# Key and input units of the near half as two spans of 264 columns

## What is computed

```python
h_res = jnp.concatenate([meta_b, x], axis=1)              # 16 + 1024 rows
h = rms_norm(h_res, pre_mix_g)
proj = jnp.einsum('bld,dc->blc', h, w_in)
q1, q2, k1, k2, v, u = jnp.split(proj, ...)
q1, q2, k1, k2 = partial_rope(...)                        # rotary positions
o = diff_attention(q1, q2, k1, k2, v, lam)                # causal, 4 heads
y = s5_ssm(u, ...)                                        # state space model over all 1040 rows
```

## Time and profile before

| | |
|---|---|
| median of 3 runs | 3443.7 us (3434.99 to 3446.54) |
| profiled execution, first to last instruction | 3446.0 us; of the three run times none is marked as its own, the slowest is 3446.54 |
| PE busy | 3106.2 us, 90% of the span |
| POOL, DVE, ACT busy | 1991.6, 1673.5, 854.1 us |
| near projection of `qk` units | about 77 to 182 us from the span's start |
| heads stage | about 182 to 510 us |

### The profile page before, as it was taken

How to read it: one execution, slowest core, us unless ns; L and a number is a source line. 1 busy time by engine, 2 the same in 40 slices (tenths; PEclk the granted TensorE clock), 3 DMA queues, 4 the chain that set the end, 5 groups by cost and what they waited for, 6 DMA issues and landing times.

```text
span 3446.0 us, 47777 instructions
## 1 busy us (share of the span) xinstructions
PE 3106.2 (90%) x19536; PEld 2393.9 (69%) x19536; DVE 1673.5 (49%) x2264; ACT 854.1 (25%) x1591; POOL 1991.6 (58%) x1076
## 2 busy tenths in 40 slices
PE   6987878799998879989999989998999988999997
PEld 4765646577776657767777767776777766788875
DVE  5844543444442551666656553646565564222333
ACT  3111123322221341123332223122323332100012
POOL 5820322554654656746665747755666765677872
PEclk9888889899999989999999999998999999999998
DMA  4343323222222434322221244332222222332231
GB/s 154 114 130 97 102 71 110 89 68 80 74 68 80 141 133 151 104 74 74 84 81 59 84 153 140 118 95 74 84 71 85 79 71 68 128 98 92 92 104 55
DMA packets 158027, 329.99 MB, mean 96 GB/s; under 512 B 34960, under 2 KB 74064, under 8 KB 157808
## 3 DMA queue, kind: packets, MB, share of 16 engines
q1 hardware_dynamic: 58752, 213.94, 19.2%
q10 hardware_dynamic: 99056, 112.99, 10.2%
HBM read 281.89 MB, written 44.97 MB: 95 GB/s over the span
## 4 chain that ended last, share of the span: by engine, by line
PE 76%; DVE 15%; ACT 3%; ACTq 2%; issue 2%; DMA 1%; POOL 0%; DVEq 0%
PE ps L1814 31%; PE ps L1855 12%; PE ps L1843 12%; PE ps L1665 2%; DVE acc_dense L2250 2%; PE ps L1576 2%; PE ps L1546 1%; DVE act_lo L2250 1%; DVE xn_dense L2257 1%; DVE ffh_lo L2930 1%; PE ps L2049 1%; DVE added L2250 1%; ACTq L965 1%; PE ps L1586 1%; PE ps L1693 1%
## 5 line engine op out<-in xcount | busy, mean ns | idle before, releaser
L559 POOL TENSOR_TENSOR w_hi<-w_raw,ones 128x1024 fp32r<-128x1024 f32 x408 | 805.6, 1975 | 1175.9 <-DMA w_raw<-weights 1172.7
L561 POOL TENSOR_TENSOR w_lo<-w_raw,w_hi 128x1024 fp32r<-128x1024 f32 x408 | 1019.3, 2498 | 32.0
L1814 PE MATMUL ps<-act_hi,w_hi 128*128 128x512 f32 x1696 | 703.9, 415 | 13.6 <-ACT qk_raw L674 8.1
L1814 PE MATMUL ps<-act_lo,w_hi 128*128 128x512 f32 x1696 | 678.4, 400 | 0.0
L1814 PE MATMUL ps<-act_hi,w_lo 128*128 128x512 f32 x1696 | 674.5, 398 | 0.0
L1814 PEld LDWEIGHTS ps<-act_hi,w_hi 128*128 128x128 f32 x1696 | 324.1, 191 | 108.5 <-issue 16.6
L1814 PEld LDWEIGHTS ps<-act_hi,w_lo 128*128 128x128 f32 x1696 | 323.7, 191 | 75.0
L1814 PEld LDWEIGHTS ps<-act_lo,w_hi 128*128 128x128 f32 x1696 | 324.1, 191 | 67.0 <-issue 1.7
L2250 DVE TENSOR_TENSOR acc_dense<-acc_dense,ps 128x512 f32<-128x512 f32 x352 | 242.0, 688 | 227.9 <-PE ps L1843 179.0
L1843 PE MATMUL ps<-w_hi,ffh_hi 128*128 128x512 f32 x704 | 296.1, 421 | 55.9 <-DVE acc_dense L2250 54.4
L1843 PE MATMUL ps<-w_hi,ffh_lo 128*128 128x512 f32 x704 | 282.4, 401 | 0.0
(11 more groups left out here) (371 smaller groups left out, 4389.1 us busy)
## 6 DMA issues: line engine op xcount, KB each, us to landing
w_raw<-weights SPq DMA_DIRECT2D x408, 512.0 KB, 3.5
rw<-rw_t ACTq DMA_DIRECT2D x24, 256.0 KB, 2.4
rw<-lora_t ACTq DMA_DIRECT2D x24, 256.0 KB, 2.0
row<-x ACTq DMA_DIRECT2D x8, 512.0 KB, 3.9
row_dense<-x ACTq DMA_DIRECT2D x8, 512.0 KB, 5.5
row_mix<-res ACTq DMA_DIRECT2D x8, 512.0 KB, 7.5
res<-row_mix ACTq DMA_DIRECT2D x8, 512.0 KB, 5.0
acc_dense<-res ACTq DMA_DIRECT2D x8, 512.0 KB, 5.6
```

What stands on the lines that cost most here:

```text
L559: pool.tensor_tensor(w_hi[:, s], raw, ones[:, 0:1].to_broadcast([P, 1024]), MUL).then_inc(w_hi_made, 1)
L561: pool.tensor_tensor(w_lo[:, s], raw, w_hi[:, s].bitcast(F32), SUB).then_inc(w_ready, 1)
L1814: mm = pe.matmul(out, ws[w][:, s, P * k:P * k + P], acts[a][:, k, x], start=(k, w, a) == (0, 0, 0), stop=(k, w, a) == (KT - 1, 1, 0))
```

## The change

`SPANS` has four entries: near 512, far 512 and two new ones of 264 columns, (0, 264) and (264, 528), that together are meta and near. Keys and inputs use spans 2 and 3 in place of 0 and 2. `rotate` and `rope_span` follow with the same spans; the count of items and steps doesn't change. In the heads stage each of the new products is two pieces of 12 matmuls, so a `u` unit's near part has 4 pieces in place of 5, and the stage has 81 pieces in place of 85.

```diff
-    SPANS = ((META, META + BANK), (META + BANK, L), (0, META))
-    spans_of = lambda m: (0, 2) if m >= 4 else (0,)
+    CUT = NEAR // 2
+    SPANS = ((META, NEAR), (NEAR, L), (0, CUT), (CUT, NEAR))
+    spans_of = lambda m: (2, 3) if m >= 4 else (0,)
+
+    def turned_beside(m, s):
+        before = spans_of(m - 1) if m else ()
+        if len(before) == 1:
+            return before if s == spans_of(m)[0] else ()
+        return tuple(b for b in before if b == s)
...
-    FAR = [("u", m, s) for m in range(4) for s in (0, 2)] + ...
-    FAR_PIECES = sum(1 if s == 2 else 4 for _, _, s in FAR) + 1
+    FAR = [("u", m, s) for m in range(4) for s in (2, 3)] + ...
+    far_pieces = lambda s: 2 if s >= 2 else 4
+    FAR_PIECES = sum(far_pieces(s) for _, _, s in FAR) + 1
...
-                if kind == "qk" and m and s in spans_of(m - 1):
-                    rotate(m - 1, s)
+                if kind == "qk":
+                    for before in turned_beside(m, s):
+                        rotate(m - 1, before)
...
-            for k in range(KT) if s == 2 else range(2 * part, 2 * part + 2):
+            each = KT // far_pieces(s)
+            for k in range(each * part, each * part + each):
```

More of the change, by code:

```diff
@@ L157, in build @@
     ROPES = len(PROJ) - QK_STEP
-    FAR = [("u", m, s) for m in range(4) for s in (0, 2)] + [("u", m, 1) for m in range(4)] + [("v", i, 1) for i in range(HALF, NT)] + [("qk", m, 1) for m in range(8)]
+    FAR = [("u", m, s) for m in range(4) for s in (2, 3)] + [("u", m, 1) for m in range(4)] + [("v", i, 1) for i in range(HALF, NT)] + [("qk", m, 1) for m in range(8)]
     FAR_U = 12
-    FAR_PIECES = sum(1 if s == 2 else 4 for _, _, s in FAR) + 1
+    far_pieces = lambda s: 2 if s >= 2 else 4
+    FAR_PIECES = sum(far_pieces(s) for _, _, s in FAR) + 1
     def ends_unit(kind, m, s):
@@ L184, in rope_index @@
     def rope_index(m, s):
-        return m + max(0, m - 4) + s // 2
+        return m + max(0, m - 4) + (s == 3)
     TB, TG, TQ = 8, 4, 2
@@ L749, in project @@
                 else:
-                    if m >= 2 and s == 0:
+                    if m >= 2 and s == spans_of(m)[0]:
                         store_turned(m - 2)
@@ L772, in project_far @@
                     store_far(m - 2)
-                if s != 2:
-                    for part in range(3):
-                        yield
+                for part in range(far_pieces(s) - 1):
+                    yield
                 if kind == "u":
@@ L778, in project_far @@
                         load_inputs(m - 1)
-                    if s != 2:
+                    if s != 3:
                         spills_landed(m % 2)
@@ L782, in project_far @@
                     c0, c1 = SPANS[s]
-                    o0, o1 = {0: (META // OCT, NEAR // OCT), 1: (0, BANK // OCT), 2: (0, META // OCT)}[s]
+                    o0, o1 = {1: (0, BANK // OCT), 2: (0, CUT // OCT), 3: (CUT // OCT, NEAR // OCT)}[s]
                     src = ps[:, n % 2, 0:c1 - c0].rearrange("p (c s) -> p c s", s=OCT)
                     give(fn(u_t[:, m % 2, :, o0:o1].rearrange("p s c -> p c s"), src, ACT.Copy), proj_kept)
-                    if s:
-                        first, last = (0, NEAR // OCT) if s == 2 else (NEAR // OCT, NOCT)
+                    if s != 2:
+                        first, last = (0, NEAR // OCT) if s == 3 else (NEAR // OCT, NOCT)
                         spill(t["u_scratch"][m][:, :, first:last], u_t[:, m % 2, :, 0:last - first], m % 2)
@@ L1526, in project_far @@
                     pe.wait_ge(proj_kept, free)
-                for part in range(1 if s == 2 else 4):
+                for part in range(far_pieces(s)):
                     if kind == "u":
@@ L1541, in far_inputs @@
             pos, (c0, c1) = AT[0, U_SSM + m], SPANS[s]
-            if s == 0 and part == 0:
+            if s == 2 and part == 0:
                 pe.wait_ge(w_ready, pos + 1)
-            for k in range(KT) if s == 2 else range(2 * part, 2 * part + 2):
+            each = KT // far_pieces(s)
+            for k in range(each * part, each * part + each):
                 for w, a in PASSES:
@@ L1547, in far_inputs @@
                                    start=(k, w, a) == (0, 0, 0), stop=(k, w, a) == (KT - 1, 1, 0))
-            if s == 2 or part == 3:
+            if part == far_pieces(s) - 1:
                 post(mm, unit_done if s == 1 else proj_psum)
@@ L1571, in feature_product @@
             u, (c0, c1) = AT[0, U_QK + m], SPANS[s]
-            if s == 0:
+            if s == spans_of(m)[0]:
                 pe.wait_ge(w_ready, u + 1)
@@ L2298, in project @@
                     dve.wait_ge(const_landed, 16 * 7)
-                if kind == "qk" and m and s in spans_of(m - 1):
-                    rope_span(m - 1, s)
+                if kind == "qk":
+                    for before in turned_beside(m, s):
+                        rope_span(m - 1, before)
                 yield
@@ L2307, in project_far @@
             for kind, m, s in FAR:
-                if s != 2:
+                for part in range(far_pieces(s)):
+                    if kind == "qk" and m and part == 2:
+                        rope_far(m - 1)
                     yield
[L2310 to L2315, removed]
             rope_far(7)
```

## The result

The changed kernel takes 3465.8 us (median of 4 runs, 3464.0 to 3474.3) and the kernel before 3441.9 (4 runs, 3435.0 to 3446.5). The ratio is 1.0077, with a 95% interval of 1.0057 to 1.0096: **24 us slower**, where I forecast 11 us faster. The profiled execution took 3464.0 us, its span is 3462.2.

The account below looks back on a forecast made before the run. PE was taken to bound the kernel (76% of the chain), with DVE pacing the near half to 160 us. Gains 3.7 + 0.6 + 2.9 + 4.2 = 11.4 us took the median 3443.7 to 3432.3 us; range 3423 to 3442.

Parts of the forecast that it names:

- The price of a product: Near-half key and input products: 0.127 us per 264-column matmul at full clock; full PE saving perhaps some 20 us.
- DVE paces the near half up to 160: Near projection: DVE has no gap until unit 4's second rotary sum near 160.2; about 0.6 us of PE's saving stays.
- Far stage at 178.5: End of the near projection: the far stage begins at 178.5 us, 3.7 us sooner.
- 1.3 us for the clock and POOL's split together: Near projection's end: allowance added for PE's low clock after idling and POOL splitting beside DVE's last sums.
- First 8 pieces, 0.6 saved: Start of the heads stage: 96 matmuls at 12.2 us plus 2.6 for the half-clock start, against 15.6 before.
- 7.3 us ahead at 231.6: Heads stage after attention steps 0 to 3: about 7.3 us gained, DVE's `frames` operations binding next.
- The turned output that I forecast near 224: Heads stage: attention's first turned output, at 231.55 before, comes near 224 us.
- 4 pieces of 6 matmuls are gone from the spread-out rest ... 4.2 us: Later heads stage: 45 pieces instead of 49, 1.39 us each; three quarters of 5.6 counted, 4.2 us saved.
- the store of `frames`: From 231.6 to 300 us: new order puts the first far product's store ahead; wait moves to next unit, nothing counted.
- The load shows at 264 columns: Rival for all narrow products: 0.218 us per matmul, PE's eight units cost 19 us more; 3457 us, chance 0.08.
- The changed order in the heads stage hurts, a few us at most: Heads-stage rival: `u_in` loads precede ACT's copies that attention awaits; counted within the rival of chance 0.32.
- The sum: Whole kernel: 3.7 + 0.6 + 2.9 + 4.2 = 11.4 us gained.

Follow-up runs that it names:

- the run with 85 pieces: Changed kernel with input units' 264-column spans cut in 3 + 2 pieces, not 2 + 2, so later pieces stand beside the same steps as before; 3429.0 us, ratio 0.9991.
- 85 pieces with later splits: Changed kernel, input spans cut 3 + 2; POOL splits unit 17 after the near half's last rotary sum, 21 after attention unit 4's first row maximum; 3426.0 us, fastest version.
- later splits: Changed kernel, 81 pieces; POOL splits units 18 and 19 after DVE's frames, 23 to 25 after attention unit 7's first row maximum; 3455.4 us, ratio 1.0043.
- the run with keys alone: Kernel before with 264-column spans only for near-half key products; inputs keep 512 + 16 columns and 5 pieces; 3436.8 us against 3438.7, ratio 1.0001.
- one step earlier: Kernel before, its 49 pieces behind step 13 all one attention step earlier, nothing removed or narrowed; 3482.5 us, ratio 1.0124.

## Why the prediction was wrong, step by step

- **The price of a product: right in the main.** Steps of 264 columns in the kernel after, at the full clock, are 0.12 us, and 0.22 at the half clock (183.25, 183.47, 183.69), where I took 0.127. PE's busy time fell by 14.5 us, of the 16 to 20 that I had:

```profile
136.03 0.28 PE L1586 MATMUL ps<-act_hi,w_lo 128*128 128x264 f32 x1
136.15 0.28 PE L1586 MATMUL ps<-act_hi,w_hi 128*128 128x264 f32 x1
136.27 0.28 PE L1586 MATMUL ps<-act_lo,w_hi 128*128 128x264 f32 x1
```

- **DVE paces the near half up to 160: right in kind.** PE waits for DVE's `qk_raw` before 148.64 and again before 162.22 (3.11 and 2.37 us); in the run with 85 pieces it is one wait of 6.64 before 160.86. I had said 160.3, and one idle time of 5 us or more. Of the ten executions with these instructions five show one wait and five show two.
- **Far stage at 178.5: missed, 182.89.** I had 1.3 us for the clock and POOL's split together; the split alone takes 2.15. Rows of the kernel after:

```profile
179.27 0.44 DVE L2260 TENSOR_TENSOR ps<-ps,rope 128x264 f32<-128x264 f32 x1 [0.94 <-PE ps L1609]
179.74 2.58 DVE L2260 TENSOR_TENSOR qk_raw<-qk_raw,rope 128x264 f32<-128x264 f32 x1
```

  POOL beside them:

```profile
177.56 2.06 POOL L568 TENSOR_TENSOR w_hi<-w_raw,ones 128x1024 fp32r<-128x1024 f32 x1 [2.39 <-DMA w_raw<-weights]
179.69 2.34 POOL L570 TENSOR_TENSOR w_lo<-w_raw,w_hi 128x1024 fp32r<-128x1024 f32 x1
```

  The other 1.9 us are the start at 162.22 in place of 160.3. Both parts show in the other runs. Where unit 17 is not held back, the stage starts at 181.2 to 182.0 in the four executions with one wait, and at 182.9 to 183.3 in the four with two; where it is held back, at 179.15 and 180.84. So the split costs some 2 to 3 us and the second wait some 1.7, and which of the two patterns comes is not set by the instructions. The kernel before had 182.30, so 3.7 us sooner became 0.6 later; but the six executions with the near half of before lie between 182.3 and 186.2, so a single pair is a poor measure here.
- **First 8 pieces, 0.6 saved: wrong sign.** From the first far matmul to the first row maximum it is 18.8 us, before 16.4. In all kernels with these eight pieces it is 17.3 to 20.4, in all with the eight of before 16.1 to 18.8. (My sum had a slip as well: 12.2 and 2.6 make 14.8, which is 0.8 under 15.6 and not 0.6.) The third product waits for its bank, since ACT issues DMAs before it copies the first: `[2.70 <-ACT u_t L683]` at 193.10. This stands on rows alone.
- **7.3 us ahead at 231.6: right only with the pieces at their places.** With 85 pieces unit 2 stands at 226.25, and with later splits too at 226.06, 6.8 and 7.0 ahead of before. In the changed kernel the far units end two steps sooner, units 18 and 19 are split beside `frames`, and it is 6.5 late. (Here too a slip: 3.7 and 4.0 make 7.7 where I wrote 7.5, and I took 7.3 where PE's own sum gave 7.2.) These rows are of the kernel after, DVE:

```profile
226.09 5.01 DVE L2260 TENSOR_TENSOR frame_tmp<-frames 128x512 f32<-128x512 f32 x2
...
232.06 1.62 DVE L2260 TENSOR_TENSOR small<-small 128x1 f32<-128x1 f32 x1
233.72 2.46 DVE L2263 TENSOR_SCALAR e_br<-e_br,small 128x144 f32<-128x144 f32 x1
```

  The turned output that I forecast near 224 comes at 237.02.
- **"4 pieces of 6 matmuls are gone from the spread-out rest ... 4.2 us": the step that failed.** I priced the pieces that were gone, at 1.39 us each, and not the 45 that stayed. 36 of them moved, by up to five steps (the last nine stand where they did), and up to 34 us hang on where they stand. The stretch from unit 4 on lost 23 us. The order of instructions shows each moved piece, and I had used it only for the end of the near half and the store of `frames`.
- **The rivals.** "The load shows at 264 columns" was the only one that ended slower, and its mechanism didn't come. "The changed order in the heads stage hurts, a few us at most" was the right kind of cause, at a tenth of its price and in the wrong stretch. The loads of `u_in` that it named were isolated in no run; what the runs isolated is POOL's splits and DVE's rotary sum. The reason for its low price was wrong: of ACT's busy time (11.64 of 68.40 us) I concluded that its place could not matter. An engine's busy share doesn't say what its queue holds back.
- **The sum.** The narrow products bring 12 us in the stage at fixed places, and 11.4 were forecast, for a change that was not made alone. That the two agree is partly luck. I had 7.2 us up to 231.6 and 4.2 behind it, for pieces that were gone; with 85 pieces none is gone, 10.0 us stand at unit 4 already, and the 1.9 behind it are within the scatter.

## What to carry to other kernels

Where background work is dealt out in pieces over the steps of another loop, a change in the number of pieces is a change of the whole schedule. Keep the count (cut the shorter work in as many pieces) or compare for each later piece which step it stands beside; price the pieces that move, not those that go. When two engines' work has the same period as here, four pieces and four steps, try the whole set one step earlier and later before anything finer. And when a slot comes free earlier, ask what starts then, and beside what: here a wait on the engine that had time made the kernel faster (later splits: 227.8 us from unit 4 on in place of 236.7).

## What the runs showed of the hardware

DVE's operations with both inputs in SBUF stand still while a split of POOL runs: 0.43 us became 2.58 (179.74 to 182.32) beside a split from 179.69 to 182.03, four scans 1.81 became 8.80. The operation just ahead, with an input in PSUM, took its 0.44 us beside a split as well. This is what the Trainium skill ("SBUF — State Buffer", Who interferes with whom) describes as an exclusive lock: against a GpSimd operation that reads SBUF, a DVE operation with two SBUF inputs that starts second waits for its end. By that rule, each half of a split that starts first can hold DVE for its full 1.9 or 2.4 us; the 2.15 us at 179.74 agree.

The schedule can repeat itself to 0.1 us. From unit 4 to the last row maximum, 214 us, the 85 pieces with later splits stayed 13.9 to 14.0 us ahead of the kernel before, in another execution. It need not: the run with keys alone, with the same pieces, is 3.4 us behind the kernel before at unit 10, 1.1 at unit 12 and 2.25 at the last row maximum. Over this stretch the six profiles with the places of before lie within 3.5 us, while the rest of the kernel scatters by 18 us. So a single profile resolves this stretch to a few microseconds, enough for effects of 10 to 30 us and not for one of 2.

The stage's granted clock is lower where the places are bad, as the table of all runs shows: 0.88 to 0.90 in the fast ones, 0.78 to 0.85 in the others. The fixed window of 300 to 510 us cuts the stage elsewhere in each run and is less clean (0.86 in the fastest version). The lower clock has its price: from unit 4 on the same 821 matmuls keep PE busy for 181.1 us before and for 194.1 us one step earlier, 13.0 of the 29.4 us. It comes with PE's waits, and no run tells how much of it would be left without them. The fixed window with 85 pieces, and one step earlier:

```profile
300.00:510.00 210.00, 170.41 (x782) 117.71 (x783) 108.18 (x209) 48.73 (x137) 51.58 (x24) 0.89 0.29 86
```
```profile
300.00:510.00 210.00, 171.69 (x734) 120.63 (x731) 102.50 (x189) 35.12 (x112) 42.90 (x20) 0.82 0.26 79
```
